# Early query weights out of the raw ring: two buffers of their own in tiles that are idle then

## The reference

```python
ada = jax.nn.silu(c) @ lp['w_ada'] + lp['b_ada']
sh1, sc1, g1, sh2, sc2, g2 = [a[:, None, :] for a in jnp.split(ada, 6, axis=-1)]
mix, states = mixer(x * (1 + sc1) + sh1, attend, conv_buf, h0, lp)
x = layer_norm(ALPHA * x + (1 + g1) * mix, lp['ln_g'][0], lp['ln_b'][0])
gt, up = jnp.split((x * (1 + sc2) + sh2) @ lp['w_ffn_in'], 2, axis=-1)
f = (jax.nn.silu(gt) * up) @ lp['w_ffn_out']
```

## Time and profile before

| | |
|---|---|
| median of three runs | 1800.41 us |
| the profiled execution, its own time | 1797.79 us |
| its span, first to last instruction | 1796.1 us |
| TensorE busy / VectorE busy / ScalarE busy | 97% / 49% / 38% |
| moved by DMA | 384.00 MB, mean 214 GB/s |
| granted clock of TensorE, mean | 0.985 |

### The profile page before, as it was taken

One profiled execution on the slowest core, in us unless ns is written; L12 is line 12 of the kernel. 1 busy time (PEld: TensorE's weight loads), 2 busy tenths in 40 slices (PEclk: granted clock), 3 DMA queues, 4 the chain that ended last, 5 costly groups with the idle time before them and its releaser, 6 DMA issues.

```text
span 1796.1 us, 33174 instructions
## 1 busy us (share of the span) xinstructions
PE 1743.2 (97%) x13610; PEld 1615.1 (90%) x13610; DVE 880.3 (49%) x1379; ACT 684.3 (38%) x822; POOL 162.7 (9%) x271
## 2 busy tenths in 40 slices
PE   7888999998999999999999999999999999999997
PEld 3558888888999998889998899999999999999997
DVE  2233336654665655455783344444444444444566
ACT  1122226664444444323463333333333333333334
POOL 0001312203232411100000000000000000000001
PEclk9989999999999999999999999999999999999999
DMA  9998767656454546775546654434455444443542
GB/s 356 357 396 297 275 250 299 269 211 248 165 200 147 205 165 261 292 317 208 184 189 254 281 198 159 170 141 156 169 179 182 170 159 170 159 161 129 169 159 95
DMA packets 63747, 384.00 MB, mean 214 GB/s; under 512 B 9341, under 2 KB 9725, under 8 KB 27678
## 3 DMA queue, kind: packets, MB, share of 16 engines
q1 hardware_dynamic: 52848, 349.80, 52.1%
q0 software_dynamic: 10208, 32.32, 5.5%
q10 hardware_dynamic: 590, 0.44, 0.1%
HBM read 373.48 MB, written 9.03 MB: 213 GB/s over the span
## 4 chain that ended last, share of the span: by engine, by line
PE 86%; DMA 7%; DVE 3%; ACT 3%; issue 1%; POOL 0%; SPq 0%; POOLq 0%; ACTq 0%; DVEq 0%
PE bank L691 24%; PE bank L693 24%; PE bank L692 24%; DMA raw<-in_w_units 6%; PE bank L698 4%; PE bank L735 2%; DVE wlo L368 2%; PE bank L715 1%; ACT whi L361 1%; PE bank L859 1%; PE bank L982 1%; DMA mgate<-mg 1%; PE bank L895 1%; ACT z L1473 0%; PE bank L926 0%
## 5 line engine op out<-in xcount | busy, mean ns | idle before, releaser
L691 PE MATMUL bank<-xhi,wlo 128*128 128x288 f32 x2544 | 759.6, 299 | 11.0 <-DVE wlo L368 5.8
L692 PE MATMUL bank<-xlo,whi 128*128 128x288 f32 x2544 | 751.8, 296 | 0.0
L693 PE MATMUL bank<-xhi,whi 128*128 128x288 f32 x2544 | 749.7, 295 | 0.0
L368 DVE TENSOR_TENSOR wlo<-raw,whi 128x2048 fp32r<-128x2048 f32 (+2 forms) x234 | 491.1, 2099 | 457.9 <-ACT whi L361 455.6
L361 ACT CAST whi<-raw 128x2048 fp32r<-128x2048 f32 (+2 forms) x234 | 409.4, 1750 | 421.4 <-PE bank L693 298.6
L691 PEld LDWEIGHTS bank<-xhi,wlo 128*128 128x128 f32 x2544 | 478.1, 188 | 26.0 <-issue 20.4
L693 PEld LDWEIGHTS bank<-xhi,whi 128*128 128x128 f32 x2544 | 480.4, 189 | 0.0
L692 PEld LDWEIGHTS bank<-xlo,whi 128*128 128x128 f32 x2544 | 479.0, 188 | 0.5
L693 PE MATMUL bank<-hhi,whi 128*128 128x288 f32 x704 | 208.8, 297 | 0.0
L691 PE MATMUL bank<-hhi,wlo 128*128 128x288 f32 x704 | 208.4, 296 | 0.2 <-DVE wlo L368 0.2
L692 PE MATMUL bank<-hlo,whi 128*128 128x288 f32 x704 | 205.3, 292 | 0.0
(11 more groups left out here) (333 smaller groups left out, 1704.7 us busy)
## 6 DMA issues: line engine op xcount, KB each, us to landing
raw<-in_w_units SPq DMA_DIRECT2D x278, 1024.0 KB, 5.7
raw<-in_w_ffn_out_units SPq DMA_DIRECT2D x64, 704.0 KB, 4.0
raw<-in_w_units SPq DMA_DIRECT2D x8, 896.0 KB, 8.4
mgate<-mg POOLq DMA_DIRECT2D x32, 144.0 KB, 2.6
mgl<-mgate POOLq DMA_DIRECT2D x16, 288.0 KB, 6.3
bz<-relrow POOLq DMA_DIRECT2D x16, 192.0 KB, 3.4
xt<-in_x SPq DMA_DIRECT2D x8, 288.0 KB, 6.4
z<-in_x POOLq DMA_DIRECT2D x4, 576.0 KB, 8.8
```

What stands on the lines that cost most here:

```text
L368: nc.vector.tensor_tensor(wlo[e][:, 0:size], raw[:, s, 0:size], f32(whi[e][:, 0:size]), ALU.subtract).then_inc(raw_used[s], 1)
L691: pe.matmul(acc, wt[1][:, w], x[0][:, c, :], start=start, stop=False)
L692: pe.matmul(acc, wt[0][:, w], x[1][:, c, :], start=False, stop=False)
L693: return pe.matmul(acc, wt[0][:, w], x[0][:, c, :], start=False, stop=stop)
```

## The change

Stage `INIT` becomes 32 A units and nothing else, so the ring carries conditioning units alone in that phase. The pieces of the early query weights come from an input of their own (`w_early`), with contiguous rows of 1792, and go in turn to two buffers `eraw`, the first 1792 columns of the idle tiles `kvT` and `yv`, with semaphores of their own. The load of piece q is issued in the middle of period q's A units instead of behind them. ScalarE's split of a piece moves from behind `a_copy` of its period to ahead of it, VectorE's from between `mod_full` and `mod_low` to ahead of `a_out` (in period 0 both keep their place; in period 7 both stood ahead already). On TensorE the six groups are spread as 2, 2, 1 and 1 instead of 3, 2 and 1, and the last group stands behind the turn.

```diff
-INIT = Stage("AAAAG" * 7 + "GAAAA", 1, 0, 0, 0)
-EARLY = 7
-QS = Stage("AAGGAA", 1, INIT.r_end, INIT.g_end, INIT.a_end)
+INIT = Stage("A" * 32, 1, 0, 0, 0)
+EARLY, EIGHTHS = 7, 8
+QS = Stage("AAGGAA", 1, INIT.r_end, EIGHTHS, INIT.a_end)
...
+        PIECE = EARLY * 2 * P
+        eraw = [kvT[:].rearrange("p k g t -> p (k g t)")[:, 0:PIECE], yv[:].rearrange("p c t -> p (c t)")[:, 0:PIECE]]
+
+        def early_hi(act, q):
+
+            act.wait_ge(e_in[q % 2], 16 * (q // 2 + 1))
+            after(act, unit_done, q - 1)
+            nc.scalar.copy(whi[q % 2][:, 0:PIECE], eraw[q % 2]).then_inc(hi_done, 1)
+
+        def early_lo(dve, q):
+
+            dve.wait_ge(hi_done, q + 1)
+            nc.vector.tensor_tensor(wlo[q % 2][:, 0:PIECE], eraw[q % 2], f32(whi[q % 2][:, 0:PIECE]),
+                                    ALU.subtract).then_inc(e_used[q % 2], 1)
...
-            for pos in range(INIT.U):
-                if pos in INIT.A:
+            def early_load(q):
+
+                sp.dma_start(xt[:, 2 * q:2 * q + 2, :], a["x"][:, 2 * q:2 * q + 2, :]).then_inc(x_in[q % 2], 16)
+                after(sp, e_used[q % 2], q // 2)
+                sp.dma_start(eraw[q % 2], a["w_early"][q]).then_inc(e_in[q % 2], 16)
+
+            for q in range(EIGHTHS):
+                for pos in range(4 * q, 4 * q + 4):
                     load(INIT, 0, pos, first=pos < RAW_SLOTS)
-                else:
-                    q = pos // 5
-                    sp.dma_start(xt[:, 2 * q:2 * q + 2, :], a["x"][:, 2 * q:2 * q + 2, :]).then_inc(x_in[q % 2], 16)
-                    s, k = INIT.raw(0, pos)
-                    sp.wait_ge(raw_used[s], k)
-                    sp.dma_start(raw[:, s, 0:EARLY * 2 * P], a["w_units"][pos][:, 0:EARLY * 2 * P]).then_inc(raw_in[s], 16)
+                    if pos % 4 == 1 and q:
+                        early_load(q)
+                if q == 0:
+                    early_load(0)
...
                     if g == 0:
                         pe.wait_ge(mod_lo, q + 1)
-                        s, k = INIT.rawG(0, q)
-                        pe.wait_ge(raw_used[s], k + 1)
+                        pe.wait_ge(e_used[q % 2], q // 2 + 1)
...
-                early_unit(q - 1, (0, 1, 2))
+                early_unit(q - 1, (0, 1))
                 a_units(INIT, 0, (4 * q + 2,))
-                early_unit(q - 1, (3, 4))
+                early_unit(q - 1, (2, 3))
                 a_units(INIT, 0, (4 * q + 3,))
+                early_unit(q - 1, (4,))
+                a_turn(q)
                 early_unit(q - 1, (5,))
-                a_turn(q)
...
             for q in range(8):
-                if q == 7:
-                    split_hi(act, INIT, 0, q, EARLY * 2 * P)
+                if q:
+                    early_hi(act, q)
                 a_copy(INIT, 0, q)
-                if q < 7:
-                    split_hi(act, INIT, 0, q, EARLY * 2 * P)
+                if q == 0:
+                    early_hi(act, q)
                 mod_high(0, xm, q, q % 2)
...
-                if q == 7:
-                    split_lo(dve, INIT, 0, q, EARLY * 2 * P)
+                if q:
+                    early_lo(dve, q)
                 a_out(q)
...
-                if q < 7:
-                    split_lo(dve, INIT, 0, q, EARLY * 2 * P)
+                if q == 0:
+                    early_lo(dve, q)
                 mod_low(0, xm, q, q % 2)
...
-        "w_units": units, "w_ffn_out_units": fo, "x": feat(x), "cond": feat(c),
+        "w_units": units, "w_early": np.ascontiguousarray(first), "w_ffn_out_units": fo, "x": feat(x), "cond": feat(c),
```

More of the change, by code:

```diff
@@ L309, in build @@
         raw_used = [sem(f"raw_used{s}") for s in range(RAW_SLOTS)]
+        e_in, e_used = [sem("e_in0"), sem("e_in1")], [sem("e_used0"), sem("e_used1")]
         hi_done = sem("hi_done")
@@ L1576, in _ @@
             split_lo(dve, QS, 0, 0)
-            dve.wait_ge(unit_done, INIT.g_end)
+            dve.wait_ge(unit_done, EIGHTHS)
             for u in range(EARLY):
@@ L1580, in _ @@
                 if u < 2:
-                    ins.then_inc(acc_free[u], INIT.g_end // 2)
+                    ins.then_inc(acc_free[u], EIGHTHS // 2)
             split_lo(dve, QS, 0, 1)
@@ L2049, in lay_out @@
     first = bq[:EARLY].reshape(EARLY, P, DC // 2, 2, P).transpose(2, 1, 3, 0, 4).reshape(DC // 2, P, -1)
-    first = np.concatenate([first, np.zeros((DC // 2, P, UNIT - EARLY * 2 * P), np.float32)], 2)
     gates = np.concatenate([wg[:, gcols], np.zeros((D, P - 48), np.float32)], 1)
@@ L2069, in woven @@
         return out_
-    units = np.stack(woven(INIT, first, wa) + woven(QS, [blocks(gates)[0], bq[EARLY]], wa) + woven(KVS, blocks(wkv), wa)
+    units = np.stack(woven(INIT, [], wa) + woven(QS, [blocks(gates)[0], bq[EARLY]], wa) + woven(KVS, blocks(wkv), wa)
                      + woven(RNN, wr, wa) + list(blocks(wm)) + woven(CMB, comb, wa) + list(wo) + woven(FIRST, ff, wa) + woven(NEXT, ff[4:], wa) + list(ff[16:]))
```

## The result

The changed kernel took 1783.7 us, the median of four runs (1780.54 to 1785.91), against 1800.04 us for the kernel before beside it: a ratio of 0.9911, with a 95% interval of 0.9891 to 0.9931. That is faster by 0.9%, and lies 1.3 us under the lower end of the forecast range.

What follows compares the result with a forecast made beforehand. The prediction took transfers with holes at 402 GB/s to bound the first phase. Piece 7 starting 10.4 us sooner gave 1787.4 us, or 1790.0 by the runs' median; it forecast 1789 (1787 to 1791), with a wider range of 1785 to 1796.5.

Steps and rivals of the forecast that it cites:

- What bounds the phase, and the holes: First 130 us: bound by transfers; holes from pieces keeping ring slots lose 2.90 MB, 7.2 us, and would close from 4 us on.
- the 56.1 us: SP's wait for VectorE's split of a G unit before the change, read as the source of the holes.
- The rate of the full ring: First phase: the full ring moves 402 GB/s, so a period's 5.41 MB take 13.5 us.
- my sum: Start of piece 7 moves from 130.09 to 119.7 us, 10.4 us gained, giving 1787.4 us.
- The path behind it: End of `INIT`: last A unit at 113.4 us, bias at 116.3, second `QS` unit at 118.6, piece 7 at 119.7 us.
- A core's share of HBM: Skill's figure of some 358 GB/s would put the second `QS` unit at 133 us, no gain; the trace's 402 spoke against it.
- The splits and the group behind the turn: `INIT`: splits moved ahead save 1.1 us from bias to `xlo`; the group covers TensorE's 0.3 to 0.4 us at the bias.
- Behind piece 7: After piece 7 TensorE bounds; first `QS` G unit split by 125.4 us, needed at 126.2; the 3.9 us `KVS` wait stays.
- The clock fell once: Rival 1: a lower TensorE clock in period 7 takes part of the gain, leaving 7 to 8 us, 1792; chance 0.20.
- A stream under 386 GB/s: Rival 2: the full ring is slower; at 380 GB/s 3.7 us gained, 1796.5, within 0.3% of no change; chance 0.15.
- a clock low in every period: Rival 3: stalls bring half rate in every period of the first phase, 1806; chance 0.06 with all else slower.
- rival 4: More than the sum: the 3.9 us wait in `KVS` goes too, gain 14 us, 1785.5; chance 0.07.

## Why the prediction fell short

**What bounds the phase, and the holes.** Right. The holes at 24, 48 and 84 us closed, and the change did what the first two paragraphs say. One reading there is too large: the 56.1 us of the earlier trace rows are over 200 us. Up to 104 us, where the first stage's loads end, SP's waits for VectorE's split are 30.7 us, six in number.

**The rate of the full ring.** This is the step that failed, by its size: "A period's transfer is [...] 5.41 MB, or 13.5 us at 402 GB/s", and the same 402 placed every event. I took a DMA share of 1.00 for the best that the stream can do. It did 418 GB/s over 100 us, and the turns came 13.05 us apart (21.16 to 112.51 us, seven periods). The third A unit of the last period, 43.3 MB in all with the 1.1 MB of other loads, would come at 4 plus 42.93 by 402, 110.8 us; it came at 107.4. That is 3.4 us, and the start of piece 7 missed by 3.2 (116.48 against 119.7).

The trace of the kernel before could have shown it. The 402 of the earlier trace rows is a mean over 40 us. In slices of 4 us (columns as above) the same trace has

```profile
60.00:64.00 4.00, 4.00 (x34) 2.58 (x27) 0.00 (x0) 0.33 (x1) 0.00 (x0) 1.00 1.04 429
64.00:68.00 4.00, 2.54 (x22) 1.57 (x20) 2.28 (x6) 2.51 (x3) 0.00 (x0) 1.00 1.00 424
76.00:80.00 4.00, 4.00 (x34) 2.57 (x26) 0.00 (x0) 0.33 (x1) 0.00 (x0) 1.00 0.99 366
92.00:96.00 4.00, 3.37 (x31) 2.08 (x23) 1.06 (x5) 2.17 (x2) 0.00 (x0) 1.00 1.01 428
```

and seven of its 25 slices from 28 to 128 us move 419 to 429 GB/s. The changed kernel moves 400 GB/s or more in every slice from 4 to 120 us but one.

Three loads ahead instead of four bring the rate back to 387 GB/s at a share of 0.99, so the rate hangs on how many loads SP may have under way. By that run one may suspect the same of the kernel before, since a piece in the ring left three slots for A units. Of the two parts, fewer places and holes, only the second was in my sum.

**The path behind it.** In part another than I had. I let two transfers set it: the last A unit at 113.4 us for the bias, and the second A unit of `QS` at 118.6 us for piece 7. In the run TensorE's last wait for a load was for the third A unit, at 107.43 us. From there it was busy up to the turn; the bias began at 113.50 us, `xlo` ended at 116.43, 2.9 us later as in the prediction, and let piece 7 start. The two units of `QS` ran from 114.42 us without a wait for a load. With 418 in place of 402 my sum puts the second unit of `QS` at 114.2 us and piece 7 at 115.3, 1.2 us too early. So the rate alone is worth 4.4 us, TensorE's own work took 1.2 of it, and that the miss of 3.2 is so near the 3.4 of the third A unit is partly luck.

**A core's share of HBM.** The Trainium skill, DMA: Bandwidth & Descriptors, Specifications, gives some 358 GB/s, half of what it has for a stack that two cores share. 418 GB/s over 100 us, in six runs with one core at work, are against it as a limit for a core that works alone; the 435 GB/s of the same section for the fabric were not exceeded.

**The splits and the group behind the turn.** The text says that the group "pays nothing except in the last period", and prices the splits by the last period. Wrong as a statement on the parts. I had compared the 11.0 us of TensorE's work with 13.5 us of transfers, and left out what stands between pieces of work: the bias (0.36 us) and the low part (1.92 us). With them the old order needs 13.2 us a period, more than the 12.9 that the transfers take once the ring is free. Buffers alone start piece 7 at 121.19 us. In the changed kernel the orders are both new, one period (61.89 to 73.26 us, turn to turn) is 11.4 us long with 0.23 us of wait for a load in it, and so the sum was right to go by the transfers up to the last period.

**Behind piece 7.** Right: the first G unit of `QS` began 6.5 us after piece 7 (122.99 less 116.48), as before, and the wait in `KVS` moved along.

**The rivals.** The clock fell once, 0.86 in 48 to 60 us, and not in the last period; the next period was 11.4 us long and won the time back. A stream under 386 GB/s did not come, a clock low in every period neither. More than the sum did come, but not by rival 4, whose wait stayed at 4.0 us. I had no rival for a stream faster than in the trace of before, though the earlier trace rows show 389 to 405 GB/s at shares of 0.99 to 1.01, a spread that should have told me that the share does not fix the rate.

**The range.** Its lower end of 1785 was 1.3 us too high. Of the 5.3 us between 1789 and the measured 1783.7, 3.2 are the miss at piece 7, and 1.6 come from setting the forecast above the sum's 1787.4. With the 3.2 us at piece 7, the sum is 1784.2 from the profiled execution's own time; the measured 1783.24 of the changed one is within the scatter of what lies behind piece 7.

## What to carry to other kernels

A full DMA share says that packets were under way all the time, not that the engines moved as much as they can. Look at the rate in short slices as well: where the best ones lie clearly above the mean at the same share, the mean is not the limit, and more loads in flight may raise it. A piece that stays long in a small ring costs by the loads that it blocks, and, as the run with three loads ahead suggests, by the place that it takes.

When the supply gets faster, compare its period with the consumer's whole chain from turn to turn, waits for other engines included, not with the consumer's busy time. A chain that just fills the period has no slack to win back what a spell at a lower clock costs. Two ways to shorten that chain may be worth as much as one.

## What the runs showed of the hardware

One core moved 418 GB/s from HBM over 100 us, in six runs of five kernels, with four loads of 1 MB and up to two pieces allowed in flight, and 387 GB/s over 72 us with one A unit fewer, both at a DMA share within 0.03 of 1.00. I had expected the share to give it away. The cause inside the DMA engines was not tested: the median packet of 8 KB took 309 to 312 ns at either rate, and 80 packets of over 600 ns stand against 5. The limit on the loads also lets TensorE's stops reach the transfers, and this run does not part the two, least of all beyond 84 us, where the share falls to 0.94.

In a chain of TensorE that was 13.2 us at the full clock, a spell at the lower clock made a period 14.6 to 14.8 us long.
